# The sparse part of the PEER loop one step behind the dense part

## The reference, cut to what matters

```python
def one_block(xb):
    ...
    eidx = jnp.take_along_axis(cidx, pos, axis=-1)
    gate = jax.nn.softmax(top_s, axis=-1)
    act = jax.nn.gelu(jnp.einsum("nd,nhkd->nhk", xb, u_tab[eidx]).astype(jnp.float32))
    coef = (gate * act).astype(xb.dtype)
    return jnp.einsum("nhk,nhkd->nd", coef, v_tab[eidx])
...
x = x + g2 * peer(h, peer_wq, peer_keys, peer_u, peer_v)
...
return (rmsnorm(x, norm_f), ...)
```

## Time and profile before

| | us |
|---|---|
| median of 3 runs | 3148.6 (3148.13 to 3150.77) |
| the profiled execution | 3148.99 |
| its span, first to last instruction | 3147.2 |

### The profile page before, as it was taken

One profiled execution on the slowest core, in us unless ns is written; L12 is line 12 of the kernel. 1 busy time (PEld: TensorE's weight loads), 2 busy tenths in 40 slices (PEclk: granted clock), 3 DMA queues, 4 the chain that ended last, 5 costly groups with the idle time before them and its releaser, 6 DMA issues.

```text
span 3147.2 us, 46544 instructions
## 1 busy us (share of the span) xinstructions
PE 2948.0 (94%) x15708; PEld 2351.6 (75%) x15708; DVE 2525.7 (80%) x5697; ACT 812.6 (26%) x1592; POOL 1505.9 (48%) x1211
## 2 busy tenths in 40 slices
PE   6999899899998577599999999999999999999997
PEld 2566464467776466588888888888888888888886
DVE  6371324448999999589999999999999999999998
ACT  3213220144445599211111111111111111111112
POOL 0000000007676100466776667777667676777662
PEclk8989999999999699799999999999999999999998
DMA  5012641289999476999999999999999999999996
GB/s 206 6 54 42 183 136 56 106 312 336 327 338 318 163 199 183 378 372 387 396 390 396 391 389 391 392 396 390 394 386 395 394 391 389 392 395 390 390 394 251
DMA packets 343600, 959.32 MB, mean 305 GB/s; under 512 B 37168, under 2 KB 135520, under 8 KB 333360
## 3 DMA queue, kind: packets, MB, share of 16 engines
q0 software_dynamic: 147456, 536.94, 43.5%
q1 hardware_dynamic: 175264, 412.59, 36.7%
q10 hardware_dynamic: 20784, 8.67, 1.1%
HBM read 841.10 MB, written 116.85 MB: 304 GB/s over the span
## 4 chain that ended last, share of the span: by engine, by line
PE 82%; DVE 7%; ACT 4%; DMA 3%; issue 2%; ACTq 1%; POOL 0%; SPq 0%; DVEq 0%
PE ps L945 31%; PE ps L934 25%; PE ps L825 6%; PE ps L791 4%; PE ps L706 4%; PE ps L808 2%; DMA arena<-in_w_ada 2%; ACT arena L1236 2%; PE ps L656 2%; ACT arena L1253 2%; DVE arena L1692 1%; DVE arena L1341 1%; PE ps L741 1%; DVE arena L1823 1%; DVE arena L1687 1%
## 5 line engine op out<-in xcount | busy, mean ns | idle before, releaser
L945 PE MATMUL ps<-w,v_rows 128*128 128x320 f32 (+1 forms) x4096 | 1033.6, 405 | 0.0
L945 PEld LDWEIGHTS ps<-w,v_rows 128*128 128x128 f32 x4096 | 763.1, 190 | 203.2
L579 POOL DMA_INDIRECT ring<-in_vt,arena x512 | 701.5, 1370 | 285.9 <-DVE y_rows L1854 191.2
L579 POOL DMA_INDIRECT ring<-u_table,arena x512 | 560.1, 1094 | 457.1 <-DVE ring L1840 216.1
L934 PE MATMUL ps<-h_hi,u_hi 128*128 128x320 f32 (+1 forms) x2048 | 653.3, 319 | 33.3 <-DVE u_lo L1341 31.5
L1854 DVE SCALAR_TENSOR_TENSOR y_rows<-ring,s5c,y_rows 128x1024 f32<-128x1024 f32 x512 | 652.4, 1274 | 1.4 <-DMA ring<-in_vt,arena 1.2
L1840 DVE SCALAR_TENSOR_TENSOR ring<-ring,h_rows 128x1024 f32<-128x1024 f32 x512 | 623.3, 1218 | 16.5 <-DMA ring<-u_table,arena 10.0
L934 PE MATMUL ps<-h_hi,u_lo 128*128 128x320 f32 (+1 forms) x2048 | 607.1, 296 | 0.0
L934 PE MATMUL ps<-h_lo,u_hi 128*128 128x320 f32 (+1 forms) x2048 | 606.8, 296 | 0.0
L1275 ACT ACTIVATE w<-ps 128x320 f32<-128x320 f32 (+1 forms) x256 | 104.6, 410 | 1235.0 <-PE ps L934 1112.6
L934 PEld LDWEIGHTS ps<-h_hi,u_hi 128*128 128x128 f32 x2048 | 389.6, 190 | 40.3 <-DVE u_lo L1341 31.9
(11 more groups left out here) (239 smaller groups left out, 3021.8 us busy)
## 6 DMA issues: line engine op xcount, KB each, us to landing
u_turn<-in_ut SPq DMA_DIRECT2D x128, 512.0 KB, 5.6
u_table<-u_turn SPq DMA_DIRECT2D x128, 512.0 KB, 4.2
u_raw<-in_ut SPq DMA_DIRECT2D x128, 512.0 KB
v_rows<-in_vt SPq DMA_DIRECT2D x64, 1024.0 KB
c_raw<-coef_dram SPq DMA_DIRECT2D x64, 576.0 KB
coef_dram<-arena SPq DMA_DIRECT2D x8, 4096.0 KB, 15.9
arena<-in_w_ada SPq DMA_DIRECT2D x16, 1024.0 KB, 8.9
arena<-in_w_ada SPq DMA_DIRECT2D x4, 2048.0 KB, 13.1
```

The source lines that it names most:

```text
L579: nc.gpsimd.indirect_dma_start(out=slot(n), out_offset=None, in_=table, in_offset=bass.IndirectOffsetOnAxis(ap=uvi[:, at:at + 1], axis=0)) ...
L945: last = mm(ps[4 + m % 4][:, 0:width], seg(v_in_buf, 2048 * r + 1024 * e + P * d, P), seg(w_in_buf, ow, width), start=n == 0, stop=n == 3)
```

## The change

Everything sparse in step t is renumbered by one: DVE takes the dots of sparse step t-1 (before t) and the weights and row additions of t-2 (before t-1), and ACT's gelu at the end of `act_step(t)` is that of the dots of t-1. The lists of POOL, SP and PE have the same instructions in the same order. What differs in kind is what stands ahead of the loop and behind it.

```diff
+            def dots_gelu(g, u):
+                act.wait_ge(s("u_rows_done"), 8 * g + 8)
+                av(acts[:, u, :], dots[:, u, :], ACT.Gelu_apprx_tanh).then_inc(s("acts_ready"), 1)
...
-                act.wait_ge(s("u_rows_done"), 8 * t + 8)
-                av(acts[:, r % 2, :], dots[:, r % 2, :], ACT.Gelu_apprx_tanh).then_inc(s("acts_ready"), 1)
+                if not first:
+                    dots_gelu(t - 1, 1 - r % 2)
...
-                if 1 <= d < NS:
-                    square_of(d - 1)
-                if d == 5:
+                if d == 3:
+                    dots_gelu(63, 1)
+                if d == 7:
+                    for t in range(NS - 1):
+                        square_of(t)
...
-                        weights_of(t - 1, 1 - u)
+                        weights_of(t - 2, u)
...
-                        dot(t, u, p)
+                        dot(t - 1, 1 - u, p)
                         add_up(g, 8 * u + p, early)
-                        add_row(t - 1, 1 - u, p)
+                        add_row(t - 2, u, p, early and r == 2)
...
-            for p in range(8):
-                dot(0, 0, p)
-                if p == 4:
-                    u_rest(1, 0)
+            u_rest(1, 0)
             for j in range(4):
                 weigh(0, 0, j)
             u_rest(1, 1)
-            weights_of(0, 0)
             for p in range(8):
-                dot(1, 1, p)
-                add_row(0, 0, p, True)
-                if p > 3:
-                    weigh(0, 1, p - 4)
+                dot(0, 0, p)
+                if p % 2:
+                    weigh(0, 1, p // 2)
                 if p == 6:
                     u_rest(2, 0)
...
-            weights_of(63, 1)
+            weights_of(62, 0)
...
-                if m in (3, 5, 7):
-                    sparse_sum((m - 3) // 2)
+                if m < 8:
+                    dot(63, 1, m)
+                    add_row(62, 0, m)
+                if m == 8:
+                    weights_of(63, 1)
                 if m >= 8:
                     add_row(63, 1, m - 8)
-                if m == 10:
-                    dve.wait_ge(s("ssq4"), NS - 1)
...
-                if m >= 13:
-                    scaled_out(m - 13)
-
+
+            for t in range(NS - 1):
+                sparse_sum(t)
...
+            dve.wait_ge(s("roots_ready"), 7)
+            link(V.reciprocal(rms4[:, 20:23], rms4[:, 20:23]))
+            for t in range(NS - 1):
+                scaled_out(t)
```

More of the change, by code:

```diff
@@ L1921, in _ @@
                 for r in range(4):
-                    tile_of = [s4, s4 if r else s4 - 1]
+                    tile_of = [s4 if r else s4 - 1, s4 if r > 1 else s4 - 1]
                     dve_step(4 * s4, r)
@@ L1947, in _ @@
                     dve.wait_ge(s("x1_back"), 16)
-                if m in (3, 5, 7):
-                    sparse_sum((m - 3) // 2)
+                if m < 8:
[3 more added lines that the diff above has]
+                    weights_of(63, 1)
                 if m >= 8:
                     add_row(63, 1, m - 8)
-                if m == 10:
-                    dve.wait_ge(s("ssq4"), NS - 1)
[L1954 to L1959, removed]
-                if m >= 13:
-                    scaled_out(m - 13)
+            for t in range(NS - 1):
+                sparse_sum(t)
             dve.wait_ge(s("v_in0"), 16 * 16 + 32)
             sparse_sum(NS - 1)
+            dve.wait_ge(s("ssq4"), NS - 1)
+            ts(rms4[:, 10:13], rms4[:, 0:3], 1.0 / DM, EPS, ALU.mult, ALU.add).then_inc(s("mean_squares_ready"), 1)
+            dve.wait_ge(s("norm_f_in"), 16)
             for t in range(NS, NTILE):
```

## The result

The changed kernel takes 3174.84 us (median of 5 runs, 3167.21 to 3178.56) where before takes 3148.13 (5 runs, 3142.04 to 3150.77). The ratio is 1.008, with a 95% interval of 1.0065 to 1.0095: slower, by 0.8%, and outside the range of the prediction. The profiled execution, on which what follows rests, took 3167.65 us with a span of 3165.9; it is the second fastest of the five.

A forecast was written before the change was run, and what follows sets the result against it. PE sets the loop's pace, so gains must come from its two start waits, with DVE bounding the tail. The terms -7.5 - 11.7 + 0 + 11.7 + 6.8 = -0.7 gave 3147.9 us, range 3141 to 3156.5.

The forecast's parts named there:

- The loop: Loop steps: neither shorter nor longer, 0 us, since PE has no wait there and DVE's instructions per step stay the same.
- rivals A to E: Alternatives: store still blocks ACT, tail gathers in time, DMA lag, quicker gathers, no effect; chances 0.20, 0.15, 0.10, last two 0.05.
- C: First loop steps: the DMA engines fall behind and PE waits a third time; 7 us of new waiting, 3154.9 us; chance 0.10.
- The first wait: PE before the scores of step 1: ACT's store drains sooner with gathers held back; 7.5 us gained, ends 0 and 9.
- rival A: Start: the store still blocks ACT, as SP's loads alone may starve its queue; 3155.4 us; chance 0.20.
- The second wait: PE before the scores of step 2: fewer instructions ahead of `u_rest(2,0)`; 11.7 us gained, ends 10.5 and 12.9.
- L: Start: time from the gather into the first dot's slot until its own dot can start; 6.7 us, between 5.5 and 7.9.
- The tail: Behind the loop: eight more dots and row additions on DVE, 11.7 us lost; gathers competing with the `x` reload, 6.8 us lost.
- The sum: Whole kernel: start gains of 7.5 and 11.7 us against tail losses of 11.7 and 6.8 us, -0.7 us in all.

The follow-up runs named there:

- the last run: Changed kernel with 40 instructions more and x's second part reloaded after all gathers, plus `u_rest(2,0)` moved from behind the seventh dot to the fourth; 3141.96 us, ratio 0.9999.

## Why the prediction was wrong

**The loop: the step that failed.** It put the loop at 0 because DVE's instructions per step are "the same in number and place". In number they are, but for one; the place it had looked at was that within the step. The place in DVE's list had moved, by 31 to 34 instructions, and three loops of four came to lie so that DVE idles 3.3 to 8.7 us at each back edge, with five more packets on its instruction queue. The loop took 21.9 us more, and with 40 idle instructions it takes 0.0 us more. None of the rivals A to E was this one; C named the same sign and nearly the same rows (waits on `u_lo`), but another cause, another place and a third of the size.

**The first wait** was right in its cause and too small: the gain is 9.1 us against 7.5, at the end named for loads that start earlier. (The terms of that sum, 1285, 4.0 and 1, add up to 1290.0 and not to 1290.4, so it should have said 7.9. And the gathers beside the 0.14 MB, called half in rival A, were 2.0 of 5.25 MB.) How much there was to gain differs with the execution: with 256 instructions more, where ACT's issue took 15.5 us, the cast began 19.7 us after the issue did, in the kernel before 23.9 and in the changed one 14.7. ACT's issue ended 7.5 us after it began, and the cast was released by the load of `u_raw`, as forecast:

```profile
1269.45 7.52 ACTq L1288 DMA_DIRECT2D coef_dram<-arena  x3
1284.16 1.04 ACT L1229 CAST u_hi<-u_raw 128x1024 fp32r<-128x1024 f32 x1 [14.73 <-DMA u_raw<-in_ut]
```

**The second wait.** From the end of the first to the end of the second it is 23.8 us (1310.42 less 1286.61), forecast 21.7; the gain is 9.6 us, a little under the range of 10.5 to 12.9. L was sized too small: the gather of POOL at 1295.86 had its dot at 1304.12, 8.3 us, where 6.7 was taken and 7.9 was the end. A wait of 1.1 us for the gather of the seventh dot comes on top, which the sum did not have. In the run with 40 instructions more the same stretch is 22.0 us. The 3.2 us estimated by the Trainium skill (DMA: Bandwidth & Descriptors, Anatomy of one DMA) are further off still, in a stretch where the DMA engines carry other transfers. And the last run shows that there is nothing to gain by freeing `u_lo` from that gather: PE waited as long for `w`, behind another one.

**The tail** was right within 1.6 us: +20.1 against +18.5. Of its 71.53 us DVE is busy 62.48 (forecast 62.4) and idle 9.05 (forecast 0.8 and 6.8). Of the idle time 8.0 us are waits for the ring, at the second dot and the row addition behind it, not at the third dot. The four waits, in the timeline of DVE:

```profile
3097.33 1.23 DVE L1846 SCALAR_TENSOR_TENSOR ring<-ring,h_rows 128x1024 f32<-128x1024 f32 x1 [3.18 <-DMA ring<-u_table,arena]
...
3102.76 1.28 DVE L1860 SCALAR_TENSOR_TENSOR y_rows<-ring,s5c,y_rows 128x1024 f32<-128x1024 f32 x1 [4.19 <-DMA ring<-in_vt,arena]
...
3104.69 1.23 DVE L1846 SCALAR_TENSOR_TENSOR ring<-ring,h_rows 128x1024 f32<-128x1024 f32 x1 [0.24 <-DMA ring<-u_table,arena]
...
3128.11 1.29 DVE L1860 SCALAR_TENSOR_TENSOR y_rows<-ring,s5c,y_rows 128x1024 f32<-128x1024 f32 x1 [0.40 <-DMA ring<-in_vt,arena]
```

**The sum** of start and tail was right: the changed kernel with 40 instructions more, in which nothing but the fetching is taken out, has the same span as before, 3147.2 us in the profiled executions (start -20.4, loop 0.0, tail +20.3), and the interval of its ratio, 0.9998 to 1.0022, holds no difference.

**What stays open.** Three of the five runs of the changed kernel lie at 3174.8 to 3178.6 us, above the profiled 3167.65; whether they wait longer for instructions or elsewhere, no profile shows. Nor is it settled at which instruction exactly the edge lies.

## What to carry to other kernels

A loop like this one, of 292 instructions, may or may not fetch at its back edge, and an edit ahead of it, even of idle instructions, can switch that on or off: compare where each loop starts in its engine's list before and after, and read the instruction queue's packets on the page first when a wait with `<-issue` stands at the top of a loop. Work that is moved out of a start which an engine and the DMA engines fill comes back in the tail at full price (20.4 us gained, 20.3 lost), unless the tail has idle time for it. A wait that is removed on an engine with work queued behind the same transfers tends to come back under another name.

## What the runs showed of the hardware

At six back edges of a loop whose body is 292 instructions, DVE idled 3.3 to 8.7 us each, with some five packets each on the instruction queue. With 20 or 40 idle instructions ahead of the loops the gaps are gone, and 222 bring them into the other kernel while 256 do not. The loops show how much of this DVE could hide: gaps of 3.3 and 3.6 us left no wait on PE, 6.4 us left 2.6, and 8.7 us left 4.9. ACT's issue of three stores takes 7.4 to 8.4 us in nine traces, and 15.5, 21.5 and 23.9 us in the three in which six gathers of POOL's queue are issued beside it.
